# A gather of 128 rows issued as one of 120 and one of 8, once in two steps

## The reference

```python
sc = jnp.einsum('phcd,hcnd->phcn', q, sub_keys)          # 8 heads, 2 x 128 keys
top_s, top_i = lax.top_k(sc, PEER_TOPK)                  # 16 of 128, for both halves
best_s, best_pos = lax.top_k(cand_s, PEER_TOPK)          # 16 of the 256 sums
idx = jnp.take_along_axis(cand_i, best_pos, axis=-1)     # one of 16384 experts
g = jax.nn.softmax(best_s, axis=-1)
act = jax.nn.gelu(jnp.einsum('phkd,pd->phk', expert_u[idx], xb), approximate=False)
coef = g * act
out = jnp.einsum('phk,phkd->pd', coef, expert_v[idx])
```

## Time and profile before

| what | us |
|---|---|
| median of three runs | 1816.09 (1815.74 to 1816.41) |
| the profiled execution | 1816.22 |
| its span, first to last instruction | 1813.4 |
| DVE busy | 1497.3 (83%) |
| PE busy | 1574.7 (87%) |
| POOL busy | 796.0 (44%) |
| ACT busy | 352.4 (19%) |
| granted TensorE clock, mean | 0.993 of full |

### The profile page before, as it was taken

How to read it: one execution, slowest core, us unless ns; L and a number is a source line. 1 busy time by engine, 2 the same in 40 slices (tenths; PEclk the granted TensorE clock), 3 DMA queues, 4 the chain that set the end, 5 groups by cost and what they waited for, 6 DMA issues and landing times.

```text
span 1813.4 us, 18894 instructions
## 1 busy us (share of the span) xinstructions
PE 1574.7 (87%) x4808; PEld 814.2 (45%) x4808; DVE 1497.3 (83%) x3518; ACT 352.4 (19%) x970; POOL 796.0 (44%) x559
## 2 busy tenths in 40 slices
PE   7999999899989988888878888878888888788886
PEld 6888878677534333333333333333333333333332
DVE  5788987578689988888888888888888888888887
ACT  5232333456211120110100110110011101001101
POOL 1000000000044555666556666655666665466662
PEclk9999999899999999999999999999999999999999
DMA  7565472242289999999999999999999999999996
GB/s 304 186 228 187 179 274 93 62 176 70 93 355 421 421 421 421 421 419 422 421 419 410 419 413 421 422 422 422 406 407 422 422 422 421 422 398 422 422 421 254
DMA packets 93679, 623.93 MB, mean 344 GB/s; under 512 B 11440, under 2 KB 11440, under 8 KB 24240
## 3 DMA queue, kind: packets, MB, share of 16 engines
q0 software_dynamic: 78912, 570.46, 76.5%
q1 hardware_dynamic: 14704, 52.74, 7.9%
HBM read 621.06 MB, written 2.10 MB: 344 GB/s over the span
## 4 chain that ended last, share of the span: by engine, by line
DMA 42%; PE 34%; DVE 10%; issue 6%; POOL 4%; DVEq 2%; ACT 1%; POOLq 0%; ACTq 0%; SPq 0%
DMA arena<-in_experts,idx 42%; PE ps L425 8%; PE ps L426 8%; PE ps L427 8%; PE ps L645 7%; DVE arena L1389 5%; POOL arena L414 4%; PE ps L561 1%; DVE arena L1415 1%; PE ps L448 1%; DVE lnw L1283 1%; PE ps L595 0%; DVEq L1265 0%; DVEq L1281 0%; PE ps L534 0%
## 5 line engine op out<-in xcount | busy, mean ns | idle before, releaser
L645 PE MATMUL ps<-arena 128*128 128x512 f32 x2048 | 1000.7, 615 | 213.2 <-DVE arena L1415 208.8
L414 POOL DMA_INDIRECT arena<-in_experts,idx x512 | 774.8, 1513 | 683.1 <-PE ps L645 348.4
L645 PEld LDWEIGHTS ps<-arena 128*128 128x128 f32 x2048 | 352.5, 190 | 812.4 <-DVE arena L1415 550.0
L1389 DVE CUSTOM_DVE_ANT_0 arena<-arena 128x1024 f32<-128x1024 f32 x512 | 626.9, 1224 | 92.7 <-DMA arena<-in_experts,idx 88.5
L879 ACT ACTIVATE lnw<-lnw 128x1 f32<-128x1 f32 x512 | 103.9, 203 | 1132.3 <-DVE lnw L1389 1132.2
L1415 DVE TENSOR_SCALAR arena<-ident,lnw 128x128 f32<-128x128 f32 x512 | 170.7, 333 | 3.9 <-ACT lnw L879 3.8
L377 POOL DMA_DIRECT2D arena<-in_w_ada x24 | 12.9, 538 | 231.5 <-DVE arena L979 221.3
L425 PE MATMUL ps<-xT_hl,w_hl 128*128 128x512 f32 x192 | 76.8, 400 | 9.2 <-DVE xT_hl L942 9.2
L937 DVE TENSOR_TENSOR w_hl<-arena,w_hl 128x1024 fp32r<-128x1024 f32 x47 | 57.4, 1222 | 28.6 <-ACT w_hl L681 28.5
L426 PE MATMUL ps<-xT_hl,w_hl 128*128 128x512 f32 x192 | 75.4, 393 | 0.0
L427 PE MATMUL ps<-xT_hl,w_hl 128*128 128x512 f32 x192 | 75.4, 392 | 0.0
(11 more groups left out here) (231 smaller groups left out, 1622.4 us busy)
## 6 DMA issues: line engine op xcount, KB each, us to landing
arena<-in_w_ada POOLq DMA_DIRECT2D x24, 1024.0 KB, 5.4
arena<-in_w_in SPq DMA_DIRECT2D x44, 512.0 KB, 3.3
arena<-in_experts,idx POOLq DMA_INDIRECT x512
arena<-in_w_out SPq DMA_DIRECT2D x14, 512.0 KB, 5.5
lnw<-in_w_in SPq DMA_DIRECT2D x8, 512.0 KB, 4.5
arena<-in_w_grp POOLq DMA_DIRECT2D x4, 1024.0 KB, 7.8
arena<-in_w_out SPq DMA_DIRECT2D x1, 4096.0 KB, 12.8
arena<-in_w_q SPq DMA_DIRECT2D x1, 4096.0 KB, 12.3
```

Source lines behind the costliest of these rows:

```text
L414: nc.gpsimd.indirect_dma_start(slot(n), None, experts, bass.IndirectOffsetOnAxis(ap=idx[:, e, n:n + 1], axis=0)).then_inc(arr[n % RING], 16)
L645: last = mm(ps[half][:, :], lhsT=diag[:, n % RING, :], rhs=slot(n)[:, DM + half * T:DM + (half + 1) * T], start=(e == 0 and n == 0), stop= ...
L1389: nc.vector.tensor_tensor_reduce(out=urow, in0=urow, in1=h2[:, t, :], scale=1.0, scalar=0.0, op0=ALU.mult, op1=ALU.add, accum_out=dots[:, ...
```

## The change

The last gather of a pair of steps, (e, n) = (1, 15), is issued as two indirect DMAs. The first takes partitions 0 to 119, the second 120 to 127. The second reads its 8 indices from a new tile `idxs`, at partitions 0 to 7. They are put there by a small DMA from `idx`, issued by GpSimd once the second step's indices are ready, ahead of that step's gather 0, and waited for ahead of gather 15. Both gathers add 16 to the slot's semaphore, so slot 7 gets 80 in a pair where it got 64, and VectorE's waits are counted anew by `arrivals`. `DVE_SLOT` goes from 13 to 5.

```diff
-DVE_SLOT, ACT_SLOT = 13, 104
+DVE_SLOT, ACT_SLOT = 5, 104
+SPLIT, TAIL = (1, 15), 8
@@ in mixers_and_peer
+        idxs = sb("idxs", [P, 1], u32)
+        idxs_in = sem("idxs_in")
@@ GpSimd's loop
                 for e in range(2):
                     pool.wait_ge(idx_ready, 2 * i + e + 1)
                     pool.sem_inc(pool_go, 1)
+                    if e == SPLIT[0]:
+                        pool.dma_start(idxs[0:TAIL, :], idx[P - TAIL:P, e, SPLIT[1]:SPLIT[1] + 1]).then_inc(idxs_in, 16)
                     for n in range(TOPK):
+                        if (e, n) == SPLIT:
+                            pool.wait_ge(idxs_in, 16 * i + 16)
+                            pool.sem_inc(pool_go, 1)
                         pool.wait_ge(slot_free, 2 * TOPK * i + TOPK * e + n + 1)
                         pool.sem_inc(pool_go, 1)
+                        rows = P - TAIL if (e, n) == SPLIT else P
                         nc.gpsimd.indirect_dma_start(
-                            slot(n), None, experts,
-                            bass.IndirectOffsetOnAxis(ap=idx[:, e, n:n + 1], axis=0)).then_inc(arr[n % RING], 16)
+                            slot(n)[0:rows, :], None, experts,
+                            bass.IndirectOffsetOnAxis(ap=idx[0:rows, e, n:n + 1], axis=0)).then_inc(arr[n % RING], 16)
+                        if rows < P:
+                            nc.gpsimd.indirect_dma_start(
+                                slot(n)[rows:P, :], None, experts,
+                                bass.IndirectOffsetOnAxis(ap=idxs[0:TAIL, :], axis=0)).then_inc(arr[n % RING], 16)
@@ VectorE
+            def arrivals(s0, e, n):
+
+                if n % RING != SPLIT[1] % RING:
+                    return s0 * (16 * TOPK // RING) + 16 * (TOPK // RING * e + n // RING + 1)
+                split = 16 if (e, n) >= SPLIT else 0
+                return s0 * (16 * TOPK // RING + 8) + 16 * (TOPK // RING * e + n // RING + 1) + split
@@ two_steps
-                        dve.wait_ge(arr[n % RING], step * (16 * TOPK // RING) + 16 * (n // RING + 1))
+                        dve.wait_ge(arr[n % RING], arrivals(s0, e, n))
```

## The result

| | us |
|---|---|
| kernel before, same chip, median of 4 | 1816.25 (1815.74 to 1817.98) |
| changed kernel, median of 4 | 1913.11 (1909.97 to 1915.08) |
| ratio | 1.0529 (95% interval 1.0516 to 1.0541) |
| span of the profiled execution | 1908.0 (before 1813.4) |
| granted TensorE clock, mean | 0.966 (before 0.993) |

The forecast was 1803.5, faster. The kernel is 5.3% slower: 96.9 us, or 6.05 us for each of the 16 splits.

The account below looks back on a forecast made before the run. The prediction took one DMA engine, late by its instruction fetches, to bound the expert stage's gathers. Its terms, -20.0 + 5.0 + 1.0 + 1.3 = -12.7 us, took 1816.2 to 1803.5 us; the range was 1797 to 1818.

Parts of the forecast that it names:

- (a): Gather (1,15) with 120 rows, not 128, sixteen times: spares the late engine its 8 rows, -20.0 us (0 to 21.8).
- (b): The other 8 rows in their own gather, one row on each of eight engines: +5.0 us.
- late engine: In the expert stage, one DMA engine delayed by 23 q14 instruction fetches, 0.95 us each, 21.8 us, sets the end.
- the first rival: Relief goes round: each pair's transfers take 31 places, so each pair spares the next engine; no change, 1816 us; chance 0.18.
- (c): The copy of 8 indices, 16 times, on the DMA engines: +1.0 us (0 to 5.0).
- (f): GpSimd's added wait ahead of gather 15: the copied indices land long before it, so zero.
- (d): The 11 q8 packets on other engines, hidden until now behind the late engine: +1.3 us (0 to 1.9).
- (e): GpSimd issues 32 more DMAs, 33 us in all, hidden under the queue: zero.
- (g): Four more register instructions in VectorE's loop body, some 0.4 us a pair, hidden in its wait for gathers: zero.
- VectorE's need: VectorE's products in the expert stage need 2.34 us a gather, 0.14 less than it gets, so no bound yet.
- a bad split of 120: 120 rows dealt to eight engines, 15 each: 4.7 us a gather, +35 us, 1851; chance 0.04 together with (f)'s wait.

## Why the prediction was wrong

**The step that failed.** It is the assumption under (a) and (b) that a row costs an engine 0.311 us wherever it goes, so that the change could be summed in rows an engine. That number was measured on transfers of 128 rows only, and holds for these. A gather of 120 rows moves fewer bytes and takes nearly twice as long: 2.0 to 2.2 us more each where sixteen stand in a row, at a busy share of 0.99. One such gather in each pair costs 91.4 us, with no short gather anywhere, where the forecast had a gain. Shown: the long gather does it, and not the copy, the wait or the code's place; and a row's time hangs on the partitions written, with the same source rows and count (64 rows, low against mid).

The mechanism that fits all runs is this. That some partitions share their way in is read from the runs; how rows are dealt to engines stands in no row and is argued. A whole gather is dealt so that each engine writes partitions that no other writes near. A shorter one is dealt in runs of neighbouring rows: eight an engine for 120, seven for 112, four for 64. Partitions 0 to 31 and 32 to 63 share their way in, which fits the 64 rows low against mid (0 to 63 take the time of 128, 32 to 95 don't). Dealt in runs, two engines write there at the same time, each at half speed, and that would be the 246 and 215 GB/s at a share of 1. A way in shared by each half of 64 partitions would also explain low against mid, but not 120 rows in runs of eight, which would load the halves with eight and seven engines.
The Trainium skill (DMA: Bandwidth & Descriptors, The descriptor swizzle) says that in a transfer to 128 partitions each engine writes one port. By the page this holds for 128; these runs show what a worse spread costs, a factor of two for 64 rows.

**The other half of the price.** Of about 6 us a split, some 2 are the long gather's own by the estimate above. Where 64-row gathers to the low half stand sixteen in a row, they cost about what whole ones do (512 KiB at 208 GB/s are 2.52 us, against 2.484), and yet the kernel is 52.3 us slower, 3.3 a pair. A single one of 60 rows in the middle still loses about 1.5. So some 3 to 4 us arise where transfers of both kinds are under way together. The explanation that fits, not shown by itself: the engines aren't in step, one is behind by its fetches and the others ahead, so a split gather is on some engines while its neighbours are on others, and they meet on the same partitions' way in. The stretched whole gathers from 751.47 on would be this. In the first pair of the stage, before one engine can have fallen far behind, the whole gathers ahead of the split are on time. How the rest divides between the gathers before and behind stays open.

**(a), the relief of 20.0.** Two things in it. A late engine is there before and after: the tail and the 23 fetches stay. But by the waits it was spared once in 16 splits and once in each sixteen of 32, not always; in this the first rival was right. With 112 and 16 or 64 and 64 rows, which divide by the 16 engines, it was never spared: 16 waits of 16. The rival's count of 31 places is not shown, for the kernel without the short gather spares it once in 16 too. Its price of no change was wrong, as it used the same 0.311.
The Trainium skill (DMA: Bandwidth & Descriptors, Why a DMA increments its semaphore by 16 and not by 1) has the cursor that goes round for transfers on fewer than 16 engines; the single product without a wait in 16, and the two in 32, agree. Its exception for some direct copies, ceil(rows / 16) rows an engine, would leave 120 rows on the first 15 engines every time, and the late engine would be spared always or never; these gathers don't follow it.

**(b), +5.0.** Behind the long gather the short one, with all else, adds 5.5 us, so the term held. Among whole gathers it measures 14 us over its rows. The rest of the price is the long one's. **(c) and (f), +1.0 and 0:** held; 0.9998 with both. **(d), +1.3:** too small to be told apart beside 97. **(e), 0:** held; the issues are two rows 1.87 us apart and GpSimd waits longer for PE's slots, not PE for GpSimd. **(g), 0:** held; with the old offset the kernel is no faster. VectorE's need, 2.34 us a gather, was about right. With 64 rows in the middle its products run from 514.68 to 1687.42 with 9.8 us of waits for gathers, (1172.7 - 9.8) / 511 = 2.28 each. This is also why that kernel gained more than expected: VectorE's pace, not that of the gathers, decides in most of both steps of a pair and not only in that of 64 rows.

**The rivals.** The slow one that had 1851, "a bad split of 120", said the right sort of thing for a wrong reason: with 15 rows on each of eight engines the other eight would have had less to do, and the share is 1.03. That its +2.2 us a gather comes near the measured 2.0 to 2.2 is luck; the 3 to 4 us at the borders it had not. The prediction gave it, together with the wait of (f), 0.04, with the reason that 15 x 8 divides as simply. It never asked where in SBUF the rows of each engine go.

Could any split gain? Sparing an engine its eight rows is worth 8 x 0.311 = 2.5 us, and each split measured costs 5.0 or more. None of the versions run beats the kernel before with all of its work.

## What to carry to other kernels

A rate per row or byte that was measured on 128-partition transfers isn't a rate for fewer partitions. Leave a tuned DMA of 128 partitions whole; a cut along its free axis was not tried here. If it has to be fewer partitions, try more than one place for them: 64 rows ran at 401 GB/s to partitions 32 to 95 and at 208 to 0 to 63. In a profile, read the DMA share beside the GB/s. In these runs a low rate at a low share was waiting (228 at 0.64 in the dip), and a low rate at a share of 1 was engines slowed by the places they wrote (208 at 1.02). And before moving load from one engine to another, find out in one run that the transfer's dealing stays on that engine.

## What the runs showed of the hardware

- 64 rows of 8 KB gathered to partitions 0 to 63 take as long as 128 rows to all partitions (208 against 421 GB/s, engines full), and to 32 to 95 about half as long (401 GB/s).
- A gather of 120 rows among whole ones costs more than its own time: 2.0 to 2.2 us more each in a row of sixteen, 5.7 more when single.
- Two gathers of 64 rows in place of one of 128 cost 5.7 us each time, 112 and 16 rows 5.0.
- With 120 rows, one split gather in sixteen is not waited for; with 112 or 64, none.
- TensorE's granted clock falls with such a stall: PE stands still from 756 to 758 and is busy for 0.58 of the next us, and then the clock goes from 1.00 to 0.50. Over the span 0.993 became 0.966, and 0.882 with 256 gathers of 120 rows.
